# Two-layer decoder trunk on one core: a head's two value chunks are moved to the end of the attention block before it, and the turns of outputs and values change places

## The reference

```python
h = rmsnorm(x, norm_g[0, 0]) * (1 + sc1) + sh1
proj = h @ w_in                                   # the q, k, v of all heads
s = einsum(q, k) - slope * distance               # causal; A heads: 4, two score maps each
w = softmax(s)[0] - lam * softmax(s)[1]           # A heads; B heads: plain banded softmax
ya = rmsnorm(w @ v, subln_g) * (1 - lam_init)
y = concat([ya, yb]) @ w_out                      # yb: 8 dilated heads of width 64
x = x + (1 + g1) * rmsnorm(y, norm_g[0, 1])
```

## Time and profile before

| what | value |
|---|---|
| three runs | 2808.80, 2813.52, 2813.25 us; median 2813.25 |
| profiled execution | 2814.57 us, its span 2812.8 us |
| PE busy in the span | 2633.5 us (94%), 12488 matmuls |
| DVE, ACT, POOL busy | 42%, 37%, 36% |
| mean granted clock of PE | 0.971 |
| stretch of the eight attention blocks | 98 to 639 us |

### The profile page before, as it was taken

One profiled execution on the slowest core, in us unless ns is written; L12 is line 12 of the kernel. 1 busy time (PEld: TensorE's weight loads), 2 busy tenths in 40 slices (PEclk: granted clock), 3 DMA queues, 4 the chain that ended last, 5 costly groups with the idle time before them and its releaser, 6 DMA issues.

```text
span 2812.8 us, 35068 instructions
## 1 busy us (share of the span) xinstructions
PE 2633.5 (94%) x12488; PEld 2150.8 (76%) x12488; DVE 1169.0 (42%) x1617; ACT 1032.7 (37%) x1676; POOL 1005.3 (36%) x436
## 2 busy tenths in 40 slices
PE   5999899989999999999999988887999999999997
PEld 3777777777788888888887777676768888888885
DVE  7476655441520154310556556556342015410045
ACT  3455543343432234322333245554443223422222
POOL 0111101004544444444444443332544444444443
PEclk9999999999999999999999989998999999999998
DMA  6233322234222222223237521111222322222223
GB/s 250 75 105 106 113 91 92 89 120 142 90 98 94 98 94 96 97 97 97 97 101 242 188 68 68 46 66 38 90 75 91 97 96 97 97 97 97 95 96 108
DMA packets 87907, 287.92 MB, mean 102 GB/s; under 512 B 9664, under 2 KB 9984, under 8 KB 87808
## 3 DMA queue, kind: packets, MB, share of 16 engines
q1 hardware_dynamic: 87808, 286.61, 30.2%
HBM read 268.75 MB, written 17.83 MB: 102 GB/s over the span
## 4 chain that ended last, share of the span: by engine, by line
PE 49%; issue 30%; POOL 10%; DVE 5%; ACT 2%; DMA 1%; DVEq 1%; SPq 1%; POOLq 0%; ACTq 0%
PE ps L592 10%; PE ps L596 10%; PE ps L593 10%; POOL w_lo L511 8%; PE ps L740 3%; PE ps L928 3%; PE ps L934 3%; PE ps L931 3%; PE ps L706 2%; PE ps L727 2%; DMA arena<-ada_w 1%; POOL ybuf L522 1%; POOL arena L522 1%; PE ps L809 1%; DMA w_raw<-weights 1%
## 5 line engine op out<-in xcount | busy, mean ns | idle before, releaser
L511 POOL TENSOR_TENSOR w_lo<-w_raw,w_hi 128x1024 fp32r<-128x1024 f32 x370 | 904.0, 2445 | 1741.3 <-ACT w_hi L998 938.2
L592 PE MATMUL ps<-h_hi,w_hi 128*128 128x512 f32 x2248 | 897.9, 399 | 29.6 <-DVE h_lo L1448 12.1
L593 PE MATMUL ps<-h_lo,w_hi 128*128 128x512 f32 x2248 | 884.1, 393 | 0.0
L596 PE MATMUL ps<-h_hi,w_lo 128*128 128x512 f32 x2248 | 558.0, 391 | 0.0
L998 ACT ACTIVATE w_hi<-w_raw 128x1024 fp32r<-128x1024 f32 x290 | 306.7, 1058 | 658.9 <-PE ps L596 362.7
L592 PEld LDWEIGHTS ps<-h_hi,w_hi 128*128 128x128 f32 x2248 | 426.5, 190 | 141.0 <-issue 23.6
L593 PEld LDWEIGHTS ps<-h_lo,w_hi 128*128 128x128 f32 x2248 | 427.6, 190 | 88.7 <-issue 2.9
L596 PEld LDWEIGHTS ps<-h_hi,w_lo 128*128 128x128 f32 x2248 | 424.4, 189 | 88.6
L1866 DVE TENSOR_TENSOR arena<-arena,ps 128x512 f32 (+1 forms) x88 | 60.6, 688 | 779.6 <-PE ps L596 779.6
L1881 DVE TENSOR_TENSOR a_lo<-arena,a_hi 128x512 fp32r<-128x512 f32 x88 | 205.4, 2334 | 206.9 <-ACT a_hi L1379 206.9
L1365 ACT ACTIVATE arena<-ps 128x512 f32<-128x512 f32 x88 | 52.7, 599 | 325.1 <-PE ps L596 325.1
(11 more groups left out here) (197 smaller groups left out, 2606.1 us busy)
## 6 DMA issues: line engine op xcount, KB each, us to landing
w_raw<-weights SPq DMA_DIRECT2D x370, 512.0 KB, 3.5
arena<-ada_w SPq DMA_DIRECT2D x80, 512.0 KB, 3.6
arena<-ada_w SPq DMA_DIRECT2D x8, 1024.0 KB, 15.0
x<-xT SPq DMA_DIRECT2D x4, 2048.0 KB, 13.4
proj<-stage SPq DMA_DIRECT2D x12, 512.0 KB, 4.5
arena<-proj SPq DMA_DIRECT2D x8, 512.0 KB, 3.7
y_hi_d<-a_hi SPq DMA_DIRECT2D x7, 512.0 KB, 2.6
y_lo_d<-a_lo SPq DMA_DIRECT2D x7, 512.0 KB, 3.9
```

Source lines behind the costliest of these rows:

```text
L511: pool.tensor_tensor(w_lo[:, s, :], w_raw[:, s, :], w_hi[:, s, :].bitcast(f32), ALU.subtract).then_inc(lo_done, 1)
L592: pe.matmul(bank(b), w, high[:, k, :], start=k == 0, stop=False)
L593: pe.matmul(bank(b), w, low[:, k, :], start=False, stop=False)
L596: mm = pe.matmul(bank(b), w_lo[:, s, k * P:(k + 1) * P], high[:, k, :], start=False, stop=k == KB - 1)
```

## The change

On PE, chunks a to a+3 stay in row blocks 0 to 3, and row block 4 has none. Chunk a+4 is cut into its three groups of eight matmuls: the first two stand at the ends of row blocks 5 and 6, the third in row block 7 between the turn of 7 and weigh(6). Chunk a+5 comes whole behind weigh(7). scores(0) of the next head moves ahead of weigh(7), scores(1) behind chunk a+5, then `turn_out`, then `turn_v`. For this, ACT and DVE process row block 0 of the next head at the end of the block, ahead of the outputs of this one; their copies of v go to the very end. ACT's copies of row block 7 now come ahead of output(6), the cast of weight unit 3b+7 moves from row block 7 to behind the eviction of chunk a+5 and ahead of L1186, and in block 6 two casts stand there. The ada steps, one for each row block before, are now none in row blocks 0 and 1, two in 2 and 3, one in each of 4 to 7.

```diff
+            def chunk_part(c, part):
+                u, half = chunk_of(c)
+                if part == 0:
+                    chunk_bank_free(c)
+                    pe.wait_ge(hi_done, u + 1)
+                if part == 2:
+                    pe.wait_ge(lo_done, u + 3)
+                w, h = ((w_hi, hh), (w_hi, hl), (w_lo, hh))[part]
+                for k in range(KB):
+                    mm = pe.matmul(bank(7), w[:, u % 2, k * P:(k + 1) * P], h[half][:, k, :],
+                                   start=part == k == 0, stop=part == 2 and k == KB - 1)
+                if part == 2:
+                    mm.then_inc(ch_done, 1)
...
-                scores(1, b, slot)
                 for n in range(8):
                     if kind == 1:
                         turn_weights(n)
+                        if n == 7 and not last:
+                            chunk_part(ahead + 4, 2)
                         if n:
                             weigh(n - 1)
...
                     if kind == 0:
                         turn_weights(n)
+                        if n == 7:
+                            chunk_part(ahead + 4, 2)
                         if n:
                             weigh(n - 1)
                     elif n > 3:
                         turn_weights(n, 1)
-                    if n < 6 and not last:
-                        chunk(6 * (b + 1) + n)
-                        if (b, n) == (6, 5):
-                            pe.drain().then_inc(unit_used, 24)
+                    if not last:
+                        if n < 4:
+                            chunk(ahead + n)
+                        elif n in (5, 6):
+                            chunk_part(ahead + 4, n - 5)
+                if not last:
+                    scores(0, b + 1, 1 - slot)
                 weigh(7)
                 if not last:
-                    turn_v(b + 1, before(LANE[kind]))
-                    scores(0, b + 1, 1 - slot)
+                    for part in range(3):
+                        chunk_part(ahead + 5, part)
+                    if b == 6:
+                        pe.drain().then_inc(unit_used, 24)
+                    scores(1, b + 1, 1 - slot)
                 turn_out()
+                if not last:
+                    turn_v(b + 1, before(LANE[kind] + 1))
...
 ACT, the end of a block
-                        if n in (5, 7) and b < 6:
-                            hi_u(3 * b + 6 + n // 6)
+                        if n == 5 and b < 6:
+                            hi_u(3 * b + 6)
                     if kind == 0:
                         load_sqrt()
+                    copies(7)
                     output(6)
-                    copies(7)
+                    if not last:
+                        evict(6 * (b + 1) + 4)
                     output(7)
...
-                        copy_v(b + 1, before(LANE[kind]))
+                        exps(b + 1, 0)
+                        evict(6 * (b + 1) + 5)
+                    if b < 6:
+                        hi_u(3 * b + 7)
+                    elif b == 6:
+                        hi_at(USE_OUT[0], 0, 0)
+                        hi_at(USE_OUT[0], 0, 1)
...
 DVE
                         if b < 7:
-                            ada_step(8 * b + n)
+                            for e in ((), (), (0, 1), (2, 3), (4,), (5,), (6,), (7,))[n]:
+                                ada_step(8 * b + e)
...
                     if not last:
                         biases((b + 1) // 4)
+                        biased((b + 1) // 4, b + 1, 0)
...
-                    if not last:
-                        copy_v(b + 1, before(LANE[kind]))
                     for half in range(2):
                         v.wait_ge(y_hi, 2 * b + half + 1)
...
+                    if not last:
+                        copy_v(b + 1, before(LANE[kind] + 1))
```

More of the change, by code:

```diff
@@ L597, in unit, with chunk_bank_free @@
                 mm.then_inc(done, 1)
-            def chunk(c):
-                u, half = chunk_of(c)
+            def chunk_bank_free(c):
                 if c > 1:
@@ L749, in turn_out @@
                     for lane in range(2):
-                        pe.wait_ge((ta_free, td_free)[lane], before(LANE[kind] + (not last)))
+                        pe.wait_ge((ta_free, td_free)[lane], before(LANE[kind]))
                         for n in range(4):
@@ L753, in turn_out @@
                         mm.then_inc((ta_done, td_done)[lane], 1)
-                scores(1, b, slot)
+                ahead = 6 * (b + 1)
                 for n in range(8):
@@ L786, in attention @@
                 scores(0, 0, 0)
+                scores(1, 0, 0)
                 for b in range(HEADS):
@@ L1112, in copy_v, with exps @@
                     a.activation(v_tok[:, 0:4, :], bank(4).rearrange("p (m q) -> p m q", q=P), ACT.Copy).then_inc(ta_free, 1)
+                def exps(b, n):
+                    for c in range(2):
+                        a.wait_ge(nm_done, 8 * b + n + 1)
+                        K = P * (n + 1)
+                        a.activation(pr[n % 2][:, c, 0:K], pr[n % 2][:, c, 0:K], ACT.Exp, bias=nmx[:, 2 * n + c:2 * n + c + 1],
+                                     accum_out=rs[:, 2 * n + c:2 * n + c + 1]).then_inc(exp_done, 1)
                 def block_(kind, b, slot, last):
@@ L1122, in copy_a @@
                         a.activation(dst, bank(4)[:, 0:m * P].rearrange("p (m q) -> p m q", q=P), ACT.Copy).then_inc(ta_free, 1)
[L1124 to L1129, removed]
                     def output(n):
@@ L1153, in copies @@
                                 copy_a(wT[n % 2][c][:, k0:k0 + m, :], m)
-                    exps(1)
+                    exps(b, 1)
                     for n in range(1, 8):
@@ L1160, in block_ @@
                         if n < 7:
-                            exps(n + 1)
-                        if n < 7 and not last:
+                            exps(b, n + 1)
+                        if n < 5 and not last:
                             evict(6 * (b + 1) + n - 1)
@@ L1183, in block_ @@
                     for half in range(2):
-                        a.wait_ge((ta_done, td_done)[half], before(LANE[kind] + (not last)))
+                        a.wait_ge((ta_done, td_done)[half], before(LANE[kind]))
                         dst = hh[half][:, b, :] if last else y_st_hi[:, half * HALF:(half + 1) * HALF]
@@ L1596, in copy_v, with biased @@
                     v.tensor_copy(v_tok[:, 4:8, :], bank(5).rearrange("p (m q) -> p m q", q=P)).then_inc(td_free, 1)
+                def biased(kind, b, n):
+                    for c in range(2):
+                        K = P * (n + 1)
+                        col = 2 * n + c
+                        v.wait_ge(s_done[c], 8 * b + n + 1)
+                        if n > 1:
+                            v.wait_ge(ta_done, events(b, lane_count(kind, n - 1, 0)))
+                            v.wait_ge(td_done, events(b, lane_count(kind, n - 1, 1)))
+                        v.sem_inc(waited, 1)
+                        v.tensor_tensor_reduce(out=pr[n % 2][:, c, 0:K], in0=ps[:, c * 1024:c * 1024 + K],
+                                               in1=bias[:, c if kind else 0, 1024 - K:1024], scale=SCORE_SCALE,
+                                               scalar=-3.0e38, op0=ALU.add, op1=ALU.max,
+                                               accum_out=mx[:, col:col + 1]).then_inc(s_read[c], 1)
+                    v.drain()
+                    v.tensor_scalar(nmx[:, 2 * n:2 * n + 2], mx[:, 2 * n:2 * n + 2], -1.0, None, ALU.mult).then_inc(nm_done, 1)
                 def block_(kind, b, last=False):
@@ L1606, in copy_d @@
                         v.tensor_copy(dst, bank(5)[:, 0:m * P].rearrange("p (m q) -> p m q", q=P)).then_inc(td_free, 1)
[L1608 to L1626, removed]
                     def copies(n):
@@ L1638, in block_ @@
                         if n < 7:
-                            biased(n + 1)
+                            biased(kind, b, n + 1)
                         if n and kind == 0:
@@ L1699, in attention @@
                 copy_v(0, 1)
+                biased(0, 0, 0)
                 for b in range(HEADS):
```

8 lines of the change are left out of this document (4 added, 4 removed).

## The result

The changed kernel takes 2827.21 us (median of 5; 2826.09 to 2829.57) against 2812.54 us (median of 5) for the kernel before: ratio 1.0052, 95% interval 1.004 to 1.0064, so 14.7 us slower. Its profiled execution has a span of 2824.4 us, 11.6 more than the one of the kernel before.

The account below looks back on a forecast made before the run. PE was taken as the bound in the attention, with only its idle time to win. A blocks +5.5, B blocks and later +2, clock +3 summed to +10.5 us on 2814.6: 2825, as median 2824, range 2809 to 2833.

Parts of the forecast that it names:

- The norm's wait goes: End of an A block: PE's 1.58 us before the turn of the outputs goes; about 0.4 remains before weigh(7).
- Row blocks 4 to 6 lose their cover: A blocks: PE idles 2.4 us before scores(7), 0.25 before the turn of 5, 2.4 before the turn of 6.
- The end of the block: A blocks: idle 1.6 us before `turn_v`, 0.1 before its second lane, 0.2 behind it; together 1.2 to 2.8.
- rival 4: Block ends: cast ahead of high parts takes back the norm's gain; without it 7 us less, 2817; no chance of its own.
- Idle time of A blocks: Blocks 0 to 3: new idle time 7.35 us against 6.0, +1.4 a block, +5.5 for four.
- What it adds in row blocks 4 to 6: A blocks: double ada steps of 1.28 us each make DVE read scores(5) some 1.4 us later; PE then waits uncovered.
- the upper end of 3.1 before scores(7): A blocks: PE's 2.4 us wait there becomes 3.1 if the double steps delay DVE by as much again.
- B blocks: Blocks 4 to 6: idle 4.4 us against 3.75, +0.7 a block, +2 for three; block 6 +1.0, block 7 wins 1.0.
- The clock: PE's clock: 2.4 us idle times twice a block in four blocks bring two or three more falls; +3, between -3 and +8.
- rival 2: A wash: waits nearer their lower ends, A blocks cost the same, clock falls no oftener; 2815; chance 0.22.

Follow-up runs that it names:

- cast_apart: Changed kernel, but ACT's cast of unit 3b+5, which starts POOL's subtraction, stands in row block 4 and not 3; 2815.2 us, ratio 1.0006.
- cast_last: Changed kernel, but the cast of unit 3b+7 (and the two of block 6) behind the outputs' high parts and the copy of v; 2835.1 us, ratio 1.0074.
- third_before_turn: As combined_cast_early, but in A blocks the last third of chunk a+4 stands ahead of the turn of row block 6; 2795.0 us, ratio 0.9937.
- combined_cast_early: As combined, but with the cast of unit 3b+7 ahead of the outputs' high parts, as in the change; 2802.6 us, ratio 0.9966.
- combined: Changed kernel with a+4 thirds in row blocks 4 to 6, casts behind high parts, ada steps in 0 to 3, 7 and behind the norm; 2801.1 us.

## Why the prediction was right, and where it was not

The direction and the range held (2824 forecast, 2809 to 2833, 2827.2 measured), and most waits came out where and as long as worked. But that the change is slower at all is luck: without a collision of POOL and DVE that the prediction didn't have, its own waits give 2815.2 (cast_apart), which can't be told from no change. Point by point:

- **The norm's wait goes.** Right: nothing stands before L771. The wait before weigh(7) was forecast at 0.4 and is 0.35, but not for the reason given: 1.30 less 0.6 and 0.6 is 0.1, and what ends the wait now is not ACT's copy but output(6) (L1171), which frees the bank.
- **Row blocks 4 to 6 lose their cover.** Right in place and in releaser. Before scores(7) 2.4 forecast, 3.31 measured; before scores(6) and the turn of 4 nothing forecast, 0.24 and 0.46 measured; before the turn of 5 0.25, measured none; before the turn of 6 2.4, measured 1.3 to 2.0, since scores(7) itself was late. Without the collision (cast_apart) the waits are 2.2 before scores(7), 0.2 before the turn of 5 and, in three of the four blocks, 2.3 before the turn of 6 (1.2 in the fourth), as the working had them (2.4, 0.25, 2.4).
- **The end of the block.** 1.6, 0.1 and 0.2 forecast; 1.52, none and 0.30 measured. But the cause that I gave for the 1.6 was wrong: cast_last moved the cast away and won only 0.24. ACT's high parts wait for the turn of the outputs, and DVE's low parts for them; the cast only delays their start a little. Of rival 4's 7 us, some 2.3 were there (0.24 to 0.30 in six blocks, 0.85 in block 6).
- **Idle time of A blocks.** +5.5 forecast, +9.9 measured, +4.6 in cast_apart. The step that failed is the first of "What it adds in row blocks 4 to 6": a step is 1.28 us, so DVE reads scores(5) some 1.4 us later. The second step of row block 3 takes 3.25. I had noted the upper end of 3.1 before scores(7) "if the double steps delay DVE by as much again", without the reason.
- **B blocks.** +2 forecast, +2.5 of idle time measured, in the places named (1.53, 0.70, 0.50, 1.37). The 0.4 forecast before the first turn of 6 isn't there; 0.45 within the second turn of 4, ended by DVE's copy, is. The two casts of block 6 cost 0.9 at its end, near the 1.0 forecast, but its second turn of 5 waits only 0.58, so that the block has no more idle time than the other two. Block 7 was forecast 1.0 shorter and is 0.2 shorter: its waits at row block 7 fell from 2.1 to 1.3, and new waits of 0.91 and 0.97 stand in its first row blocks. The rows also give DVE idle for a little under half of a B block (38.58 busy of 75.04), not "over half".
- **The clock.** +3 forecast. PE's busy time is 4.6 more in the A blocks and 1.6 less in the B blocks: +3.0. It fits in sum. Cast_apart shows +2.0 and -3.6, that is, -1.6 and not +3: the term has the wrong sign once the collision is gone, since the falls in the B blocks left, which I hadn't foreseen. That it came out was luck.

So a sum of 10.5 stands beside 14.7, with two errors of opposite sign in it: no term for the collision, which cost 12 us, and some 8 or 9 us too many for the moved cover, which without the collision costs about 2 (2815.2 against 2813.3). Without POOL's collision the change would have been within what can be told from no change (1.0006). That is the time of rival 2 of the prediction, though not its reason: the waits are not at their lower ends but where the forecast had them, and the clock gives the time back. Rival 2 lost only through a term that the prediction didn't have.

The collision is of a kind that the trace of before held, in both orders:

```profile
186.92 1.28 DVE L1579 SCALAR_TENSOR_TENSOR rinv<-arena,cs,rinv 128x1024 f32<-128x1024 f32 x1
187.31 3.15 POOL L511 TENSOR_TENSOR w_lo<-w_raw,w_hi 128x1024 fp32r<-128x1024 f32 x1 [34.58 <-ACT w_hi L1004]
...
281.17 2.66 POOL L511 TENSOR_TENSOR w_lo<-w_raw,w_hi 128x1024 fp32r<-128x1024 f32 x1 [8.88 <-ACT w_hi L1004]
282.43 1.43 DVE L1668 TENSOR_SCALAR small<-small 128x2 f32<-128x2 f32 x1
...
287.66 0.20 DVE L1674 RECIPROCAL small<-small 128x8 f32<-128x8 f32 x1 [2.44 <-ACT small L1178]
```

At 187.31 POOL's subtraction of the same unit took 3.15 us, against 2.37 elsewhere, while DVE's ada step ran to 188.20. POOL lost 0.8 where nobody waited for it. At 282.43 DVE came second: a product of two columns took 1.43 us (0.16 in the changed kernel) and ended with POOL's subtraction, at 283.8. It cost nothing, as DVE then waited 2.44 us for ACT. In the changed kernel DVE comes second where PE waits for it. The Trainium skill (SBUF — State Buffer, "Who interferes with whom") states that a DVE instruction with two SBUF inputs and a GpSimd instruction that reads SBUF exclude each other, and that whichever starts first holds the ports to its end while the other stands still. The traces agree: the loser's record ends one normal duration behind the winner's end, in either order, to within 0.2 us. The small products (L1653, L1668) read one tensor only, so the sentence above doesn't cover them; the traces show them held all the same.

## What to carry to other kernels

When a cover is moved off a stretch, lay out the engine that was hidden there with everything that its own queue and its neighbours bring, and look at POOL: an instruction with a constant duration in the old trace may be constant only because of when it ran. Read the longest record of a group beside its median, in the old trace too, before trusting the median. Put filler in front of the wait that it is to fill, in the order of the program, and not behind the work that comes after; third_before_turn won 7.6 us over combined_cast_early by that alone. And read a gain in idle time together with the granted clock, as one can take away or double the other's gain.

## What the runs showed of the hardware

- POOL's 128x1024 subtraction and DVE instructions that read SBUF twice (ada step: 1.28 to 3.25 us) or multiply two columns of SBUF by a constant (0.17 to 1.54 us) didn't run together: the one that began second took longer by the time that the other still needed. A DVE instruction with one of its two inputs in PSUM did: L1648 kept its 0.42 us beside POOL at 240.33 in cast_last.
- A collision of 2 us on an engine that is busy for less than half of the time cost 12 us of the kernel by the medians, 1.7 for each of seven places.
- The granted clock of PE in the A blocks, each in one execution, was 0.95 with 9.1 us of idle time a block (cast_last), 0.96 with 8.0, 0.97 to 0.99 with 4.4 to 7.0, and 1.00 with 3.7 (third_before_turn). More idle time did not always mean a lower clock: combined, with 5.2, had 0.99, and combined_cast_early, with 4.4, had 0.97. What decides between these two stays open.
